# The experts' down product of a hybrid encoder step: one plain fp32 matmul per block becomes three one-pass matmuls on high and low parts

## The reference, cut to what matters

```python
def moe_swiglu(h, router, wg, wu, wd):
    probs = jax.nn.softmax((h @ router).astype(jnp.float32), axis=-1)
    top_p, top_i = lax.top_k(probs, TOP_K)                    # TOP_K = 2
    ...
    for e in range(N_EXPERTS):                                # 8
        out = out + combine[..., e:e + 1] * swiglu(h, wg[e], wu[e], wd[e])

def swiglu(h, wg, wu, wd):
    return (jax.nn.silu(h @ wg) * (h @ wu)) @ wd
```

## Time and profile before

| what | value |
|---|---|
| time, median of 3 runs (lowest, highest) | 1991.38 us (1991.25, 1992.55) |
| span of the profiled execution | 1990.5 us; its own time was not given beside it, so the 0.9 us to the median are taken as what lies around the span |
| TensorE busy | 1775.2 us, 89% |
| VectorE busy | 791.9 us, 40% |
| ScalarE busy | 609.7 us, 31% |
| a routed unit | 62.5 us, ten of them from 1356 us on |
| HBM read | 329.43 MB |

### The profile page before, as it was taken

The page is one execution under the profiler, slowest core; times in us unless marked ns, Lnnn a source line. Parts: engine busy times, 40 slices in busy tenths (PEclk is TensorE's granted clock), DMA queues, the critical chain, the costliest instruction groups (busy, mean ns, idle before and its releaser), DMA issues.

```text
span 1990.5 us, 20071 instructions
## 1 busy us (share of the span) xinstructions
PE 1775.2 (89%) x7598; PEld 1222.8 (61%) x7598; DVE 791.9 (40%) x1140; ACT 609.7 (31%) x802; POOL 124.2 (6%) x243
## 2 busy tenths in 40 slices
PE   6998789878798998899977997789999999999997
PEld 3454545645678788644545475478667776667764
DVE  1611323233432333326034133246544565445653
ACT  1113112322422322210230232224443554435542
POOL 2230110000000000213002000000000000000000
PEclk9999889999899998999988999978999999999998
DMA  7534234053532333342531423536878887788873
GB/s 236 162 117 146 91 98 148 32 200 139 178 108 75 127 107 114 105 120 85 185 113 40 147 106 111 228 138 222 269 265 288 280 289 257 265 299 269 296 252 132
DMA packets 174553, 340.28 MB, mean 171 GB/s; under 512 B 6890, under 2 KB 48124, under 8 KB 174224
## 3 DMA queue, kind: packets, MB, share of 16 engines
q1 hardware_dynamic: 162224, 316.17, 46.8%
q0 software_dynamic: 3920, 12.58, 2.2%
q10 hardware_dynamic: 8352, 10.75, 1.6%
HBM read 329.43 MB, written 11.90 MB: 171 GB/s over the span
## 4 chain that ended last, share of the span: by engine, by line
PE 83%; DVE 7%; ACT 6%; issue 2%; DMA 1%; POOL 1%; ACTq 0%; SPq 0%; DVEq 0%; POOLq 0%
PE bank L924 19%; PE bank L963 12%; PE bank L964 12%; PE bank L965 12%; PE bank L1045 10%; PE bank L911 5%; PE bank L1064 3%; PE bank L941 2%; PE bank L1394 2%; DVE arena_parts L715 2%; ACT arena_parts L711 1%; PE bank L1092 1%; ACT arena L1460 1%; PE bank L1365 1%; DMA ring<-in_w_in 1%
## 5 line engine op out<-in xcount | busy, mean ns | idle before, releaser
L963 PE MATMUL bank<-arena_parts,features_parts 128*128 128x512 f32 (+1 forms) x960 | 375.8, 391 | 32.5 <-DVE arena_parts L715 21.6
L964 PE MATMUL bank<-arena_parts,features_parts 128*128 128x512 f32 (+1 forms) x960 | 369.8, 385 | 0.0
L715 DVE TENSOR_TENSOR arena_parts<-ring,arena_parts 128x2048 fp32r<-128x2048 f32 (+1 forms) x116 | 247.2, 2143 | 125.2 <-ACT arena_parts L711 125.2
L924 PE MATMUL bank<-ring,features_T 128*128 128x512 f32 (+1 forms) x672 | 273.7, 569 | 1.2 <-ACT features_T L1460 1.2
L711 ACT ACTIVATE arena_parts<-ring 128x2048 fp32r<-128x2048 f32 (+1 forms) x116 | 206.8, 1795 | 114.9 <-PE bank L965 114.1
L965 PE MATMUL bank<-arena_parts 128*128 128x512 f32 (+1 forms) x612 | 240.2, 392 | 0.0
L963 PEld LDWEIGHTS bank<-arena_parts,features_parts 128*128 128x128 f32 x960 | 184.6, 192 | 70.3 <-issue 16.6
L924 PEld LDWEIGHTS bank<-ring,features_T 128*128 128x128 f32 x672 | 128.8, 193 | 142.5 <-issue 138.1
L964 PEld LDWEIGHTS bank<-arena_parts,features_parts 128*128 128x128 f32 x960 | 184.7, 192 | 30.4
L1460 ACT ACTIVATE arena<-bank 128x512 f32<-128x512 f32 (+3 forms) x160 | 88.0, 562 | 373.7 <-PE bank L924 202.9
L965 PE MATMUL bank<-arena_parts,features_parts 128*128 128x512 f32 (+1 forms) x480 | 181.3, 378 | 0.0
(11 more groups left out here) (272 smaller groups left out, 1878.4 us busy)
## 6 DMA issues: line engine op xcount, KB each, us to landing
ring<-in_moe_w_up SPq DMA_DIRECT2D x40, 1024.0 KB, 5.1
ring<-in_moe_w_down SPq DMA_DIRECT2D x30, 1024.0 KB, 5.5
ring<-in_w_in SPq DMA_DIRECT2D x20, 1024.0 KB, 5.7
ring<-in_moe_w_gate SPq DMA_DIRECT2D x20, 1024.0 KB, 5.2
mem_kv<-in_moe_w_gate SPq DMA_DIRECT2D x20, 1024.0 KB, 5.4
ring<-in_cache_mem_k SPq DMA_DIRECT2D x16, 1024.0 KB, 6.4
ring<-in_cache_mem_v SPq DMA_DIRECT2D x16, 1024.0 KB, 5.9
ring<-in_moe_w_gate SPq DMA_DIRECT2D x20, 768.0 KB, 4.7
```

The lines of the kernel that those rows point to most:

```text
L715: nc.vector.tensor_tensor(self.part(s, 1), self.raw(s), self.part(s, 0).bitcast(F32), ALU.subtract).then_inc(self.split, 1)
L924: ins = nc.tensor.matmul(out[:, 0:w], left(k, t), wt[:, k - k0, :], start=(g == 0 and k == k0), stop=(g == len(groups) - 1 and k == k0 + n ...
L963: nc.tensor.matmul(out, left[0], right[0], start=start, stop=False)
L964: nc.tensor.matmul(out, left[0], right[1], start=False, stop=False)
```

## The change

The down product is computed as gate and up are. All 18 slabs of a unit are split. The activations' transposes are written as a high part (ScalarE) and a low part (VectorE), so VectorE now frees their bank, and their buffer doubles. TensorE uses `matmul3` for the six down slabs too. The order of the events isn't written by hand: it follows from the rule above with n_split = 18.

```diff
@@ routed_jobs
         if c:
-            jobs.append((("aT", c - 1), (T[c % 2],), "a"))
-    jobs += [(("down", 0, 0), (), None), (("down", 0, 1), (), None), (("aT", 2), (T[1],), "a"), (("down", 0), (4,), "v"),
+            jobs.append((("aT", c - 1), (T[c % 2],), "v"))
+    jobs += [(("down", 0, 0), (), None), (("down", 0, 1), (), None), (("aT", 2), (T[1],), "v"), (("down", 0), (4,), "v"),
              (("down", 1, 0), (), None), (("down", 1, 1), (), None), (("down", 1), (5,), "v")]
@@ buffers
-        actT_e = cut(f.take(FFK * P), k=FFK)
+        actT_e = parts(FFK * P, k=FFK)
@@ the loop's description
-        routed = Loop("routed", routed_jobs(), routed_slabs(), NE, ring_slots + kv_slots, ("gather", "down"),
-                      12, (0, 2, 3))
+        routed = Loop("routed", routed_jobs(), routed_slabs(), NE, ring_slots + kv_slots, ("gather", "aT", "down"),
+                      len(routed_slabs()), (0, 2, 3))
@@ TensorE, routed_step
-                        if kind == "down":
-                            ins = nc.tensor.matmul(out, left[:, k, :], wt[:, k - k0, :], start=start, stop=stop)
-                        else:
-                            ins = matmul3(out, [q[:, k, :] for q in left], [q[:, k - k0, :] for q in wt], start, stop)
+                        ins = matmul3(out, [q[:, k, :] for q in left], [q[:, k - k0, :] for q in wt], start, stop)
@@ ScalarE, routed_step
                         k0, nk = FF_GROUPS[key[1]]
-                        L.wait_filled(act, i, *key)
-                        L.emptied_by(A(actT_e[:, k0:k0 + nk, :].rearrange("p k n -> p (k n)"), b[:, 0:nk * P],
-                                       ACT.Copy), *key)
+                        L.high_part(act, i, actT_e[0][:, k0:k0 + nk, :].rearrange("p k n -> p (k n)"), b[:, 0:nk * P], *key)
@@ VectorE, routed_step
+                    elif key[0] == "aT":
+                        k0, nk = FF_GROUPS[key[1]]
+                        hi, lo = (q[:, k0:k0 + nk, :].rearrange("p k n -> p (k n)") for q in actT_e)
+                        L.low_part(dve, i, lo, b[:, 0:nk * P], hi, *key)
```

## The result

The changed kernel takes 2054.06 us (median of 4 runs, 2048.58 to 2060.29) against 1991.32 us for the kernel before (four runs on the same chip). The ratio is 1.0315, with a 95% interval of 1.0288 to 1.0342: slower by 62.7 us, where 49 were forecast. The profiled execution, with a span of 2046.7 us, was the shortest of the four; between the profiled executions of the two kernels lie 56.2 us of span. Two single executions far above the others of the same kernel, 2387 us of the kernel before and 3599 us in one experiment, are left out of all times and ratios.

The account below looks back on a forecast made before the run. TensorE was taken to bound each routed unit. Ten units times 2.8 us (waits and restarts, less savings) plus 2.1 us (clock) gave 49 us, so 1990.5 + 49 + 0.9 = 2040 us; range 2033 to 2046, with rivals 2014 to 2058.

Parts of the forecast that it names:

- its own rival of 2064 us: Clock falls at both down-product waits, so group (down 0, 1) also runs at half clock: 2.4 us more, 2064 us; chance 0.08.
- What is saved on TensorE: Down product: 66 one-pass matmuls at 0.2333 us, 15.4 us, replace 22 plain fp32 matmuls of 19.15 us, 3.75 less a unit.
- The order of the list makes two waits: Down product: aT 1 stands behind split 14, aT 2 behind split 16, so TensorE waits 2.2 us, then 4.6 us.
- The recurrence: First unit worked through engine by engine: (down 0, 1) starts at 1395.2, (down 0, 2) at 1403.0, product ends at 1413.0.
- 2.8 us a unit for waits and restarts: Down product ends later: 3.75 saved, 2.2 + (4.6 - 0.57) of waits added, 0.2 of restarts, and rounding.
- The clock falls at the second wait in every unit: After the 4.6 us wait for aT 2, TensorE's matmuls slow down, costing 2.1 us a unit (bounds 0 and 2.6).
- the middle of two rows: Clock cost of 2.1 us taken between 1.6 lost after a 3.06 us idle gap and 2.6 after one of 6.41.
- The clock at the first wait: The 2.2 us wait for aT 1 in the down product probably costs no clock; a 2.92 us gap kept 1.00.
- What follows: Scatter, gather and split 0 after the down product depend on its end alone and move with it.
- DMA at nothing: Bytes unchanged, ring slots released some us sooner, a down slab lands 7.2 us after issue, at least 12.6 ahead: no cost.
- The faster rival: Splits keep their place beside TensorE, an aT passing them in the down product: 3.1 us a unit gained, 1960 us; chance 0.08.
- Its turning point: Waits summing to 4.1 us a unit in the down product; below that the change gains, and the forecast has 6.8.

## Why the prediction was right, step by step

The direction and both mechanisms, the waits and the clock, were right. The size was short: 2054 us lies outside the forecast's own range of 2033 to 2046, and inside the wide one with the rivals, 2014 to 2058. (The top of the wide one does not cover its own rival of 2064 us.)

*What is saved on TensorE, 3.75 us a unit.* Right, and slightly low: the steps are 0.229 us in the down product where 0.233 had been taken from gate and up, so 4.0 us.

*The order of the list makes two waits.* Right in place, cause and size. Forecast were idle times of 2.2 and 4.6 us; they are 1.93 and 4.54, both ended by L724. One sign was off: when TensorE starts the second wait, at about 1399.1, it is ScalarE that is in split 16 (1398.78); VectorE waits for it and has its own part only from 1400.72. The recurrence had TensorE restart 7.8 us after the first restart (1395.2, 1403.0); it is 7.88. Moving one event took either wait away alone.

*2.8 us a unit for waits and restarts.* 2.7 measured, with the clock kept up. That it is so close is partly luck: the waits were 0.3 shorter and the saving 0.3 larger than forecast, and the later start of the product, restarts and transposes gave that back.

*The clock falls at the second wait in every unit, 2.1 us.* The fall was right, ten times of ten. The size was right on average, 22.5 us over ten units, but the single units have 1.6 to 2.65 us: in half of them this wait, of 4.5 us, cost what the one of 6.4 did. With the first wait short the same wait cost 1.3 to 2.8. So the middle of two rows hit the mean, and the spread, which no row of the kernel before showed, stays unexplained.

*The clock at the first wait, "probably not".* This is the term that failed: it had been put at nothing, from the gap of 2.92 us that kept the clock, and it measured 1.6 us in each of four units, 6.3 us in the profiled execution. There a unit is 1.0 us longer and not 1.6, as the slow stretch behind the second wait is then shorter. The rival had 2.4 us for every unit, at 0.08; four of ten is between it and the forecast.

*What follows "hangs on the end of the down product alone".* Right within the loop, and incomplete in front of it: the change also moved the gather's banks from ScalarE's to VectorE's count, so that the first gather waited for an instruction behind the routing tables, 4.9 us more in the profile. The diff had it in one letter ("a" to "v"), and I followed that letter to aT's own bank and not to the next user of the bank.

*DMA at nothing.* Right, as far as the profile tells: from the second unit on every wait of ScalarE ahead of a split (L711), 73 of them, was ended by TensorE and none by a transfer.

*The sum.* 10 x 2.7 for the waits, 4.9 for the prime and 28.8 for the clock (22.5 at the second wait, 6.3 at the first, both from the profiled execution) are 60.7 us of the 62.7; the other 2 are open. Of the 14 us between forecast and result 6.3 are the clock at the first wait, 4.9 the prime as the profile has it (its worth in the time isn't shown, see above), and 1.5 the clock at the second wait, where 21 had been put; the waits are 1 us less than forecast. The profiled execution was the shortest of four, and the others, with mean granted clocks of 0.933, 0.929 and 0.931 against its 0.933, may have lost the clock more often; no profile shows it.

*The faster rival* was right about its place: where aT passes the splits, the change gains. Its turning point was a sum of waits of 4.1 us a unit. With the clock kept up, the unit was 0.6 us shorter than before with 1.93 + 1.25 us of idle and 2.7 us longer with 1.93 + 4.54. Taken evenly between the two, the turn is at 3.8 us, an estimate.

## What to carry to other kernels

When work is added to engines that have room in sum, look at where it stands in their order: an engine that takes its instructions in turn makes a short step that the bound engine needs at once wait for every long one ahead of it, and a rule that places events by when they may run does not know when they are needed. A wait on TensorE costs more than its length as soon as the clock falls behind it (here 4.5 us of waiting and 1.6 to 2.6 on top), and work without use in the gap shows that part by itself. When the engine that frees a buffer changes, ask who uses that buffer next, in the first turn of the loop too.

## What the runs showed of the hardware that I had not expected

A wait of 1.93 us was enough to lose the clock in four of ten units of the changed kernel, in three of ten with the second wait shortened to 1.25 us, and in two of ten with matmuls in the second wait; waits of 1.25 to 1.6 us in the routed units never did, and one of 2.92 us in the kernel before had not the earlier trace rows. With aT 2 ahead of split 16, the first matmuls behind the wait of 1.93 us at 1712.93 still ran at full rate: the steps grew from 0.23 to 0.43 us only at about 1714.0, 1.0 us after the restart. The first unit of the changed kernel shows the same behind its second wait: restart at 1403.61, steps of 0.43 us from 1404.40 on, and that unit lost the least, 1.6 us.
```profile
1713.72 0.40 PE L967 MATMUL bank<-arena_parts 128*128 128x512 f32 x1
1713.95 0.47 PE L968 MATMUL bank<-arena_parts 128*128 128x512 f32 x1
1714.22 0.63 PE L969 MATMUL bank<-arena_parts 128*128 128x512 f32 x1
1714.65 0.63 PE L967 MATMUL bank<-arena_parts 128*128 128x512 f32 x1
```
